# Token tiles kept apart at the stage borders, with four buffers for the split weights

## The chip, the cores and the metric

The kernel runs on one core of a Trainium2 chip. The metric is the device time of one execution in microseconds (us), the median of the runs shown. TensorE (PE) multiplies, VectorE (DVE), ScalarE (ACT) and GpSimd (POOL) do the element-wise work, and SyncE (SP) starts the loads of the weights.

## The reference, cut to what matters

Two networks run one behind the other on 256 tokens of width 1024, all in float32.

```python
h = x
h = h + mamba2_mixer(rms_norm(h, g_pre[0]), ...)            # 32 heads, state 128, then w_out 2048 x 1024
k_nope, k_rope, v = mla_shared_kv(h, ...)                   # ckv, then kv_up 256 x 2048
cq, gate = split(rms_norm(h, g_pre[1]) @ w_in, [384])
q = (rms_norm(cq, g_q) @ w_uq)                              # uq 384 x 1536, 16 heads of 64 + 32
h = h + (causal_attention(q, k, v) * silu(gate)) @ w_out    # mla_out 1024 x 1024
h = layer_norm(rms_norm(h, g_final), ln_in)
for l in range(2):
    q, k, v, u = h @ w_in[l]                                # qk 1024 x 1024, v and u 512 each
    a = softmax(q1 k1) - lam * softmax(q2 k2)               # 8 heads; a @ v, normed per head
    f = real(fft2(u)) per group of 128, @ w_f + b_f         # 4 groups
    h = layer_norm(ALPHA * h + concat(a, f) @ w_o[l], ln1)
    h = layer_norm(ALPHA * h + (silu(h @ w_g) * (h @ w_up)) @ w_down, ln2)   # width 2816
```

## The kernel before, in words

The tokens lie in two tiles of 128 (t = 0, 1; T is 2). The weights come as 134 units of 128 x 2048 numbers, in the fixed order of `unit_plan` (L66). SP loads a unit into one of RAW (4) slots of `raw` (L404). ACT copies it, rounded, to `whi` (L1097); DVE (L1485) and POOL (L2038) each subtract one half, which gives the remainder `wlo`. These three instructions are here called the split of a unit. `whi` and `wlo` have SPL (3) slots, so the split of unit u waits until PE has used unit u - 3 (`w_used`), and SP loads unit u once DVE and POOL have split unit u - 4. Each of the three engines calls `split.until(name)` at hand-placed points of its own program; that goes AHEAD (2) units past the name. A product is three matmuls: hi x hi, hi x lo, lo x hi. `streamed` (L447) runs a whole unit, 24 matmuls for a unit of full width: first 12 for tile 0, then 12 for tile 1. `turned` (L476) gives the transposed product of a unit, 48 matmuls of 256 columns.

The stages are: the projection and convolution of the Mamba block (12 units, L570), in which DVE works out dt (`dt_second`, L1576) for a small product at CUM_AT (L586); its scan over 16 pairs of heads (L699), in which z products (L606) fill in; its output units (`acc_units`, L716); the units ckv, cq, gate, kv_up and uq (L756 to L787); latent attention over 16 heads (L842); its four output units; then twice: the units vu and qk (L912), differential attention over 8 heads with the Fourier part behind it (L1017), the four w_o units, and 11 pairs of gu units with 11 down units (L1066).

Between two stages stands a border. The sum of the output units must be read from PSUM (`add_acc`, L1734), normed (for LayerNorm `moments` L1870 on DVE, `root_ln` on POOL, `affine` L1879), turned by PE (`turn_tile`, L873), split by ACT (L1150) and DVE (L1894), and only then can the next product of that tile start (`first_pair`, L882). Before, only the last output unit of a stage reports its tile 0 early (`acc_t0`); all others run both tiles. While it waits, PE runs `keep_busy(bank, n)` (L523), n products of ones whose results nobody reads; each shows as two records at L526. In differential attention PE has 48 pieces of real products, of three matmuls each, to fill in (`side_piece`, L921): 32 of qk and 16 of vu. ACT has for each head four exponentials (L1398), one copy of transposed probabilities (L1419), and the copies of the Fourier part (L1407 to L1411); DVE has the maxima (L1941) and the combination (L1954, L1957). The w_o products wait in `o_banks` (L1036) until DVE has read the attention result (L1988 to L1992). All transposes and Fourier products go in turn through two PSUM banks, TP, and each waits until the product before the last has been copied out (`fill`, L496).

## Time and profile before

| | us |
|---|---|
| median of 3 runs | 1064.04 (1064.04 to 1066.13) |
| the profiled execution | 1063.66 |
| its span | 1061.9 |
| PE busy in it | 989.2 |
| of that at L526 (products of ones) | 69.1 |
| ACT, DVE, POOL busy | 475.3, 526.9, 521.5 |
| chain that ended last: PE, DVE, ACT | 75%, 13%, 6% |

The profile gives each instruction's start and duration. Matmuls overlap, so the time from one start to the next says more of a matmul than its own duration. PEclk is the clock granted to TensorE as a share of 2.4 GHz.

### The profile page before, as it was taken

The numbers are of one execution on the slowest core, as the hardware profiler recorded it, in microseconds if no ns is written. First come the engines' busy times: TensorE is split into PE (matmuls) and PEld (weight loads), VectorE is DVE, ScalarE is ACT, GpSimd is POOL, SyncE is SP. The second block draws the span as 40 slices with busy tenths as digits, with TensorE's granted clock in tenths as the row PEclk, the third lists the DMA queues.
The fourth block names the chain that finished last, engine by engine and source line by source line (L and its number), as shares of the span: only waits on it lengthen the run. The fifth ranks groups of instructions, "written<-read, shape, count | busy, mean of one in ns | idle before, by whom it ended". The sixth has DMA issues, their size and how long they took to land.

```text
span 1061.9 us, 13606 instructions
## 1 busy us (share of the span) xinstructions
PE 989.2 (93%) x5100; PEld 802.0 (76%) x5100; DVE 526.9 (50%) x903; ACT 475.3 (45%) x747; POOL 521.5 (49%) x240
## 2 busy tenths in 40 slices
PE   8989899898988998998989999998998989999995
PEld 6979677686867975876767888886977757888884
DVE  4697765744346647375442232236275552222324
ACT  5655644544446732474324344333375323343440
POOL 5243752573633033652445665665552544656652
PEclk9999999999989999999999999999999999999998
DMA  9444221354443024422343555554422225545520
GB/s 371 183 159 159 106 94 41 119 195 153 168 138 140 2 99 156 181 81 80 119 142 136 198 189 198 173 194 158 165 108 85 83 92 182 189 168 198 191 87 40
DMA packets 21803, 151.77 MB, mean 143 GB/s; under 512 B 2544, under 2 KB 2928, under 8 KB 3824
## 3 DMA queue, kind: packets, MB, share of 16 engines
q1 hardware_dynamic: 19872, 142.62, 38.1%
q10 hardware_dynamic: 1872, 8.34, 2.1%
q8 instruction: 41, 0.67, 0.3%
q14 instruction: 18, 0.15, 0.0%
HBM read 149.90 MB, written 1.05 MB: 142 GB/s over the span
## 4 chain that ended last, share of the span: by engine, by line
PE 75%; DVE 13%; ACT 6%; issue 3%; POOL 2%; DMA 1%; SPq 0%; POOLq 0%; DVEq 0%; ACTq 0%
PE ps L464 16%; PE ps L470 15%; PE ps L466 15%; PE ps L946 3%; PE ps L488 2%; PE ps L492 2%; PE ps L490 2%; ACT whi L1097 2%; PE ps L508 2%; DVE wlo L1485 1%; PE ps L618 1%; PE ps L963 1%; DVE res L1885 1%; DVE small L1874 1%; DVE arena L1882 1%
## 5 line engine op out<-in xcount | busy, mean ns | idle before, releaser
L2038 POOL TENSOR_TENSOR wlo<-raw,whi 128x1024 fp32r<-128x1024 f32 x134 | 427.0, 3189 | 427.7 <-ACT whi L1097 427.7
L1097 ACT CAST whi<-raw 128x2048 fp32r<-128x2048 f32 x134 | 255.9, 1912 | 194.3 <-PE ps L470 169.7
L1485 DVE TENSOR_TENSOR wlo<-raw,whi 128x1024 fp32r<-128x1024 f32 x134 | 183.8, 1372 | 292.1 <-ACT whi L1097 291.7
L464 PE MATMUL ps<-whi,ahi 128*128 128x512 f32 (+1 forms) x432 | 168.6, 390 | 8.8 <-DVE arena L2014 7.8
L466 PE MATMUL ps<-wlo,ahi 128*128 128x512 f32 (+1 forms) x432 | 168.0, 389 | 0.0
L470 PE MATMUL ps<-whi,alo 128*128 128x512 f32 (+1 forms) x432 | 162.8, 389 | 0.0
L464 PE MATMUL ps<-whi,bhi 128*128 128x512 f32 (+1 forms) x322 | 128.7, 400 | 6.7 <-issue 3.6
L466 PE MATMUL ps<-wlo,bhi 128*128 128x512 f32 (+1 forms) x322 | 125.1, 388 | 0.0
L464 PEld LDWEIGHTS ps<-whi,ahi 128*128 128x128 f32 x432 | 81.5, 189 | 27.2 <-DVE arena L2014 9.1
L470 PE MATMUL ps<-whi,blo 128*128 128x512 f32 (+1 forms) x322 | 101.7, 389 | 0.0
L470 PEld LDWEIGHTS ps<-whi,alo 128*128 128x128 f32 x432 | 81.5, 189 | 16.5
L466 PEld LDWEIGHTS ps<-wlo,ahi 128*128 128x128 f32 x432 | 81.4, 188 | 16.1
L464 PEld LDWEIGHTS ps<-whi,bhi 128*128 128x128 f32 x322 | 61.4, 191 | 21.2 <-issue 5.2
L488 PE MATMUL ps<-ahi,whi 128*128 128x256 f32 x256 | 74.1, 290 | 0.4 <-POOL wlo L2038 0.4
L490 PE MATMUL ps<-alo,whi 128*128 128x256 f32 x256 | 73.1, 285 | 0.0
L492 PE MATMUL ps<-ahi,wlo 128*128 128x256 f32 x256 | 73.0, 285 | 0.0
L470 PEld LDWEIGHTS ps<-whi,blo 128*128 128x128 f32 x322 | 61.3, 190 | 12.7
L466 PEld LDWEIGHTS ps<-wlo,bhi 128*128 128x128 f32 x322 | 61.4, 191 | 11.9 <-issue 0.5
L526 PE MATMUL ps<-ones 128*128 128x512 f32 x146 | 69.1, 617 | 1.1 <-DVE neghalf L1514 1.1
L1136 ACT CAST bhi<-ps 128x512 fp32r<-128x512 f32 x26 | 15.0, 586 | 94.4 <-PE ps L508 94.4
L1496 DVE TENSOR_TENSOR blo<-ps,bhi 128x512 fp32r<-128x512 f32 x26 | 17.8, 690 | 75.4 <-ACT bhi L1136 75.4
L488 PEld LDWEIGHTS ps<-ahi,whi 128*128 128x128 f32 x256 | 49.8, 194 | 1.2 <-POOL wlo L2038 0.6
(261 smaller groups left out, 1586.4 us busy)
## 6 DMA issues: line engine op xcount, KB each, us to landing
raw<-in_wstream SPq DMA_DIRECT2D x134, 1024.0 KB, 4.8
par<-in_params ACTq DMA_DIRECT2D x5, 1024.0 KB, 5.1
tab<-in_tables ACTq DMA_DIRECT2D x1, 1352.0 KB, 8.6
res<-in_x SPq DMA_DIRECT2D x2, 512.0 KB, 4.4
out<-res SPq DMA_DIRECT2D x2, 512.0 KB, 2.6
wfs<-in_wf ACTq DMA_DIRECT2D x1, 512.0 KB, 11.3
par<-in_params ACTq DMA_DIRECT2D x1, 512.0 KB, 12.8
arena<-in_wsmall ACTq DMA_DIRECT2D x1, 256.0 KB, 8.6
```

The source lines that it names most:

```text
L464: pe.matmul(banks[t][b][:, 0:cw], h_, wh[:, i, c], start=st, stop=False, skip_group_check=True)
L466: pe.matmul(banks[t][b][:, 0:cw], h_, wl[:, i, c], start=False, stop=False, skip_group_check=True)
L470: mm = pe.matmul(banks[t][b][:, 0:cw], l_, wh[:, i, c], start=False, stop=last and i == nks - 1, skip_group_check=True)
L488: pe.matmul(o, wh[:, k, cc], ah[:, k, :], start=(k == 0), stop=False, skip_group_check=True)
L490: pe.matmul(o, wh[:, k, cc], al[:, k, :], start=False, stop=False, skip_group_check=True)
L492: mm = pe.matmul(o, wl[:, k, cc], ah[:, k, :], start=False, stop=(k == KT - 1), skip_group_check=True)
L508: tr = pe.transpose(bank[:, k * S + t * P:k * S + (t + 1) * P], src[:, t, c0 + k * P:c0 + (k + 1) * P], ident)
L526: pe.matmul(bank, ones[:, :], ones[:, :].unsqueeze(1).to_broadcast([P, 4, P]), start=True, stop=True)
L946: mm = pe.matmul(o, a, b, start=(first and j == 0), stop=(last and j == 2), skip_group_check=True)
L1097: act.copy(whi[:, u % SPL, :], raw[:, u % RAW, :]).then_inc(w_hi, 1)
L1485: dve.tensor_tensor(wlo[:, u % SPL, c], raw[:, u % RAW, c], whi[:, u % SPL, c].bitcast(F32), ALU.subtract).then_inc(w_lo_v, 1)
L2038: pool.tensor_tensor(wlo[:, u % SPL, c], raw[:, u % RAW, c], whi[:, u % SPL, c].bitcast(F32), ALU.subtract).then_inc(w_lo_p, 1)
```

## The change: what it does

Units: RAW goes from 4 to 3, SPL (two tiles a slot) from 3 to 4 and AHEAD from 2 to 3, which takes one slot more in all; `wfs`, the Fourier weights, moves into `arena` and is loaded once for each layer.

Borders: `streamed` is built on a new `tile_products(name, t, ...)` that runs one tile of a unit. The four mla_out units and the four w_o units run all of tile 0 first, then all of tile 1 (`skew` 4); so do the last three down units of each layer, with the last transposes of the hidden layer between them. Behind the border `lead_units` does the same with four units (vu 0 to 3; gu of j = 0 and 1), and the transposes of tile 1 stand ahead of its fourth unit. DVE and POOL norm tile 0 to its end before they take up tile 1, and make the splits that the next stage needs in between. The products of ones at the borders shrink.

Fill: all four vu units move ahead of differential attention, whose loop then has 32 side pieces, and the Fourier steps move from heads 6 to 9 to heads 3 to 8. In latent attention 36 pieces (uq 1, kv_up 1, uq 2, gate 2, gate 3) go before and into the loop of the heads, with copies by ACT, rotations by DVE and splits by all three in the same loop. In the scan each pair has two z pieces instead of three; the last 16 stand behind it, in the banks G[2] and G[3]. The work for dt is spread over more units, and CUM_AT goes from 6 to 7.

```diff
-RAW, SPL = 4, 3
-AHEAD = 2
-DT_AT, CUM_AT, CB_AT = 1, 6, 9
+RAW, SPL = 3, 4
+AHEAD = 3
+DT_AT, CUM_AT, CB_AT = 1, 7, 9
...
+A_PIECES = {-1: 6, 0: 10, 1: 14, 2: 17, 3: 20, 4: 25, 5: 30, 6: 36}
+
+A_SPLITS = {0: ("uq", 1), 2: ("kv_up", 1), 4: ("uq", 2), 6: ("gate", 2), 7: ("gate", 3)}
...
-    plan += [("ckv", 0), ("cq", 0), ("cq", 1)] + [("gate", i) for i in range(4)]
-    plan += [("kv_up", i) for i in range(2)] + [("uq", i) for i in range(3)]
+    plan += [("ckv", 0), ("cq", 0), ("cq", 1), ("gate", 0), ("gate", 1), ("kv_up", 0), ("uq", 0)]
+    plan += [("uq", 1), ("kv_up", 1), ("uq", 2), ("gate", 2), ("gate", 3)]
     plan += [("mla_out", i) for i in range(4)]
     for l in range(DEPTH):
-        plan += [("vu", l, 0), ("vu", l, 1)] + [("qk", l, i) for i in QK_ORDER]
-        plan += [("vu", l, 2), ("vu", l, 3)]
+        plan += [("vu", l, i) for i in range(4)] + [("qk", l, i) for i in QK_ORDER]
         plan += [("w_o", l, i) for i in (2, 3, 0, 1)]
...
-D_SPLITS = {1: ("qk", 3), 2: ("vu", 2), 4: ("vu", 3), 6: ("w_o", 2)}
+D_SPLITS = {1: ("qk", 1), 2: ("qk", 3), 3: ("w_o", 2)}
 
 
 def side_pieces(h):
 
 
-    return (0, 12, 22, 32, 36, 40, 44)[h + 2] if h < 5 else 48
+    return (0, 12, 22, 32)[h + 2] if h < 1 else 32
 
 
 def fourier_steps(h):
 
 
-    return {6: [("pq", 0), ("f", 0)], 7: [("pq", 1), ("fy", 0), ("f", 1)],
-            8: [("pq", 2), ("fy", 1), ("f", 2)],
-            9: [("pq", 3), ("fy", 2), ("f", 3), ("fy", 3)]}.get(h, [])
+    return {3: [("pq", 0)], 4: [("f", 0), ("pq", 1)], 5: [("fy", 0), ("f", 1), ("pq", 2)],
+            6: [("fy", 1), ("f", 2), ("pq", 3)], 7: [("fy", 2), ("f", 3)], 8: [("fy", 3)]}.get(h, [])
 
 
...
-                    if n > 3 * p:
-                        scan_head(2 * p + n - 3 * p - 1)
-                    z_piece(4 + n // 4, n % 4)
+                z_piece(4 + p // 2, 2 * (p % 2))
+                scan_head(2 * p)
+                scan_head(2 * p + 1)
+                z_piece(4 + p // 2, 2 * (p % 2) + 1)
+            for q in range(12, 16):
+                z_half(q)
             pe.wait_ge(e_done, SSM_HEADS)
             pe.wait_ge(int_read, SSM_GROUPS)
-            keep_busy(X[0], 5)
...
-            def acc_units(names, ah_of, first_wait):
+            def acc_units(names, ah_of, first_wait, skew=1):
 
                 first_wait()
-                for n, (name, kts, ready) in enumerate(names):
+                whole = len(names) - skew
+                banks = [[G[0], G[2]], [G[1], G[3]]]
+                for n, (name, kts, ready) in enumerate(names[:whole]):
                     ready()
                     ah, al = ah_of(n)
-                    streamed(name, ah, al, kts, 2, D, [[G[0], G[2]], [G[1], G[3]]], n == 0,
-                             n == len(names) - 1, acc_t0 if n == len(names) - 1 else None)
+                    streamed(name, ah, al, kts, 2, D, banks, n == 0, False)
+                for t in range(T):
+                    for n in range(whole, len(names)):
+                        name, kts, ready = names[n]
+                        if t == 0:
+                            ready()
+                        ah, al = ah_of(n)
+                        mm = tile_products(name, t, ah, al, kts, 2, D, banks[t], n == 0,
+                                           n == len(names) - 1)
+                        if t == T - 1:
+                            mm.then_inc(w_used, 1)
+                    if t == 0:
+                        mm.then_inc(acc_t0, 1)
 
 
             def y_ready(i):
                 if i == 0:
...
-            pe.wait_ge(ckv_read, 1)
-            for c in range(2):
-                for i in range(2):
-                    streamed(("gate", 2 * c + i), ahi, alo, range(4 * i, 4 * i + 4), 4, 512,
-                             [[(X, G)[c][0]], [(X, G)[c][1]]], i == 0, i == 1)
             pe.wait_ge(cn_done, T)
             turn_pair(("ckv", 0), cn, 0)
+            pe.wait_ge(ckv_read, 1)
+            for i in range(2):
+                streamed(("gate", i), ahi, alo, range(4 * i, 4 * i + 4), 4, 512, [[X[0]], [X[1]]],
+                         i == 0, i == 1)
             pe.wait_ge(qn_done, T)
             turn_pair(("cq", 0), qn, 0)
             turn_pair(("cq", 1), qn, 2 * P, 1)
             wait_emptied(pe, FILL["ckv", 0])
-            for u in range(2):
-
-                if u == 0:
-                    pe.wait_ge(gate_done, 2 * T)
-                    pe.wait_ge(qn_done, T)
+            streamed(("kv_up", 0), bhi, blo, (0, 1), 2, D, [[G[0], G[2]], [G[1], G[3]]], True, True)
+            wait_emptied(pe, FILL["cq", 1])
+            pe.wait_ge(gate_done, T)
+            streamed(("uq", 0), bhi, blo, (2, 3, 4), 3, 512, [[X[0]], [X[1]]], True, True)
+
...
-                if h == 0:
-                    pe.wait_ge(mc_read, 6)
-                    keep_busy(G[2], 4)
+                if h in A_PIECES:
+                    for n in range(A_PIECES[h - 1], A_PIECES[h]):
+                        part(n)
...
+            def lead_units(names, fills, banks, acc):
 
 
                 for t in range(T):
                     wait_emptied(pe, FILL[(*fills, t, 1)])
+                    pe.wait_ge(acc_read, T * acc + t + 1)
+                        if t == 0 and i == 3:
+                            turn_tile_when(fills, 1)
+                        mm = tile_products(name, t, ahi, alo, range(4 * (i % 2), 4 * (i % 2) + 4), 4, 512,
+                                           [banks[i // 2][t]], i % 2 == 0, i % 2 == 1)
...
-                keep_busy(X[0], (10, 4)[l])
+                keep_busy(X[0], 2)
                 turn_tile_when(("h", l), 0)
-                keep_busy(X[0], (2, 3)[l])
-                pe.wait_ge(acc_read, T * (2 + 2 * l))
-                first_pair([("vu", l, 0), ("vu", l, 1)], ("h", l), [G[2], G[3]])
+                keep_busy(X[0], 2)
+                lead_units([("vu", l, i) for i in range(4)], ("h", l), [[G[2], G[3]], [G[0], G[1]]],
+                           1 + 2 * l)
+                pe.wait_ge(u_done, T * l + 1)
                 turned(("qk", l, 0), ahi, alo, G[0])
+                pe.wait_ge(u_done, T * l + 2)
...
-                for kind, g in fourier_steps(NH + 1):
-                    fourier(kind, g)
 
                 def o_banks():
-                    pe.wait_ge(u_done, T * (l + 1))
+                    pe.wait_ge(qk_done, 4 * (l + 1))
...
-                          lambda n: (bhi, blo), o_banks)
+                          lambda n: (bhi, blo), o_banks, 4)
                 pe.wait_ge(ds_max, 2 * NH * (l + 1))
-                keep_busy(X[0], 4)
+                keep_busy(X[0], 2)
                 turn_tile_when(("hm", l), 0)
-                keep_busy(X[0], 3)
+                keep_busy(X[0], 2)
+                lead_units([("gu", l, j, i) for j in range(2) for i in range(2)], ("hm", l),
+                           [[X[0], X[1]], [G[0], G[1]]], 2 + 2 * l)
 
...
+                def last_ready(d):
+                    def ready():
+                        if d == FF_UNITS - 1:
+                            ff_turn(d)
                         wait_emptied(pe, FILL["ff", l, d])
-                        k0 = 2 * (d % 4)
-                        streamed(("down", l, d), bhi, blo, (k0, k0 + 1), 2, D,
-                                 [[G[0], G[2]], [G[1], G[3]]], d == 0, d == FF_UNITS - 1,
-                                 acc_t0 if d == FF_UNITS - 1 else None)
+                    return ready
+
+                for t in range(T):
+                    for d in range(FF_UNITS - 3, FF_UNITS):
+                        name, kts = down(d)
+                        if t == 0:
+                            last_ready(d)()
+                        mm = tile_products(name, t, bhi, blo, kts, 2, D, [G[t], G[2 + t]], False,
+                                           d == FF_UNITS - 1)
```

## Rows read from the trace of the kernel before

**Rows 1.** The page: engines, L526 and the splits (count, busy us, mean ns, idle before).
```profile
PE   989.2 (93%) x5100; PEld 802.0 (76%) x5100; DVE 526.9 (50%) x903; ACT 475.3 (45%) x747; POOL 521.5 (49%) x240
L526 PE MATMUL ps<-ones 128*128 128x512 f32 x146 | 69.1, 617 | 1.1 <-DVE neghalf L1514 1.1
L2038 POOL TENSOR_TENSOR wlo<-raw,whi 128x1024 fp32r<-128x1024 f32 x134 | 427.0, 3189 | 427.7 <-ACT whi L1097 427.7
L1097 ACT CAST whi<-raw 128x2048 fp32r<-128x2048 f32 x134 | 255.9, 1912 | 194.3 <-PE ps L470 169.7
```
**Rows 2.** Windows: length, PE, PEld, DVE, ACT, POOL busy, PEclk, DMA share, GB/s.
```profile
592.70:609.50 16.80, 16.80 (x78) 13.89 (x77) 5.02 (x6) 6.76 (x6) 10.28 (x4) 1.00 0.55 188
65.80:69.20 3.40, 3.37 (x17) 3.16 (x16) 3.30 (x14) 1.29 (x3) 0.00 (x0) 0.51 0.56 200
550.50:553.90 3.40, 3.40 (x10) 2.64 (x9) 1.23 (x1) 0.27 (x1) 3.05 (x1) 0.51 0.66 193
```
**Rows 3.** Timeline, dt: start, us, instruction, count, idle before it and its releaser.
```profile
64.93 0.41 PE L586 MATMUL ps<-small,tab 128*128 128x64 f32 x2 [3.53 <-DVE small L1592]
```
**Rows 4.** Windows of the scan and behind it, and two stretches of DVE's timeline.
```profile
116.00:182.90 66.90, 63.29 (x320) 48.20 (x320) 45.81 (x52) 32.34 (x74) 34.91 (x21) 1.00 0.27 95
184.00:197.80 13.80, 11.08 (x36) 5.10 (x35) 12.29 (x18) 9.78 (x23) 10.82 (x14) 0.92 0.21 76
115.20 7.48 DVE L1661 TENSOR_TENSOR arena<-arena 128x256 f32<-128x256 f32 x4
129.84 1.43 DVE L1661 TENSOR_TENSOR arena<-arena 128x256 f32<-128x256 f32 x4
```
**Rows 5.** PE's timeline before latent attention, and the window of its loop.
```profile
300.36 0.44 PE L508 MATMUL ps<-tab,arena 128*128 128x128 f32 x2 [1.94 <-DVE blo L1502]
310.30 0.50 PE L464 MATMUL ps<-whi,bhi 128*128 128x512 f32 x1 [2.40 <-ACT arena L1331]
320.12 0.47 PE L464 MATMUL ps<-whi,bhi 128*128 128x512 f32 x1 [2.44 <-issue]
336.14 3.60 PE L526 MATMUL ps<-ones 128*128 128x512 f32 x8
340.18:372.00 31.82, 31.11 (x252) 29.54 (x253) 19.58 (x78) 23.10 (x75) 0.05 (x1) 1.00 0.01 2
```
**Rows 6.** PE's timeline at the border behind mla_out.
```profile
400.38 8.75 PE L526 MATMUL ps<-ones 128*128 128x512 f32 x20
414.36 0.47 PE L894 MATMUL ps<-whi,ahi 128*128 128x512 f32 x1 [1.13 <-issue]
418.61 1.09 PE L879 MATMUL ps<-tab,res 128*128 128x128 f32 x8 [1.27 <-DVE res L1885]
```
**Rows 7.** Differential attention, layer 0: window from head 2, an ACT group, DVE.
```profile
456.67:501.90 45.23, 41.17 (x239) 32.13 (x238) 29.40 (x80) 29.05 (x71) 18.25 (x10) 1.00 0.27 94
L1398 ACT ACTIVATE arena<-arena,small 128x256 f32<-128x256 f32 x64 | 31.8, 498 | 28.9 <-DVE small L1941 28.8
496.51 0.69 DVE L1988 TENSOR_TENSOR arena<-ps,small 128x512 f32<-128x512 f32 x1 [2.61 <-PE ps L1007]
```
**Rows 8.** PE's timeline behind w_o, layer 0; the window there in layers 0 and 1.
```profile
524.68 3.60 PE L526 MATMUL ps<-ones 128*128 128x512 f32 x8
549.55 0.50 PE L464 MATMUL ps<-whi,ahi 128*128 128x512 f32 x1 [1.82 <-DVE arena L2014]
524.70:576.20 51.50, 44.11 (x183) 32.85 (x182) 22.14 (x26) 16.43 (x16) 23.41 (x11) 0.97 0.42 143
847.40:897.40 50.00, 42.63 (x183) 31.75 (x182) 22.20 (x26) 16.43 (x16) 23.51 (x11) 1.00 0.36 127
```
**Rows 9.** The end: window behind the last product, and DVE's tile 1 chain.
```profile
1048.90:1061.90 13.00, 0.02 (x1) 0.00 (x0) 8.05 (x11) 0.00 (x0) 3.77 (x4) 0.63 0.20 81
1052.53 1.28 DVE L1742 SCALAR_TENSOR_TENSOR arena<-res,ps 128x512 f32<-128x512 f32 x2
```
**Rows 10.** The tile `raw`: time from issue to landing of the 134 loads.
```profile
DMA to landing us min/median/max: 4.6/4.8/14.5
```

608 lines of the change are left out of this document (357 added, 251 removed).

## The prediction

> **What bounds the kernel now.** I read the page first: PE is busy 93% of the span, and no other engine more than half [rows 1]. So time goes only where PE waits, runs products of ones, or runs at the lower clock. The page gives the first two: 1061.9 - 989.2 = 73 us idle and 69 us at L526, 142 us in all. The reader should see that the second lies inside the 93%. Next I laid PE's timeline out with its idle times, and cut it at the borders [rows 3, 5, 6, 8, 9]. In the steady part of the hidden layer nothing is to be gained: 16.8 us, PE busy 16.8, clock 1.00 [rows 2]. This step also gives the price list. It has 72 matmuls and two pairs of transposes of some 0.35 us, so a matmul costs (16.8 - 0.35) / 72 = 0.228 us, a unit of 24 costs 5.5, one tile of it (12) 2.74, and a piece of three 0.69. Products of ones cost 8.75 / 20 = 0.44 us a record, 0.88 a call [rows 6]. Third, windows for the clock: it falls to half (1.2 GHz) in five stretches of 3.4 us inside the work, of which the first and the last are shown [rows 2]. PE is busy throughout, so one costs 1.7 us. Ahead of the five PE had idled 3.53 us [rows 3], 1.94 and 2.40 us [rows 5], 1.82 us [rows 8], and a part of the 13.8 - 11.08 = 2.7 us behind the scan [rows 4].
>
> **The change part by part.** All against the profiled execution. "E" is the end of the products of a stage.
>
> *Convolution and dt.* PE waits 3.53 us for dt [rows 3] and pays 1.7 us of clock behind it [rows 2]. The work for dt is now spread over three units of 5.9 us, and its result is due one unit later; what DVE does per unit then stays below the 5.9. Gain 5.2 us, at worst 3.
>
> *Scan.* The window has PE busy for 63.3 of 66.9 us and DVE for 45.8 [rows 4]. 16 z pieces go out of it, 16 x 0.69 = 11.0 us, which leaves PE 52.3 us. Now DVE is at 45.8 / 52.3 = 88%, and its sequence is in order: the reading of each group of heads waits for PE, and the masks behind it wait for that. So I add 7 us of stalls (the window had 3.6; bounds 3 and 12). Then come the 11.0 us of z pieces, in which all norms fit, and the way from the first turned block to the first output unit, 197.8 - 188.9 = 8.9 us, plus two products of ones and a wait, 10.2 us. Sum 52.3 + 7 + 11.0 + 10.2 = 80.5 against 81.8 us from 116.0 to 197.8. With the clock's fall to 0.92 in that stretch [rows 4] gone (0.9 us), gain 2.2 us; bounds -3 and +6.
> The masks (L1661) show what the feeding engines do to each other: four take 1.43 us when POOL rests, and 7.48 us beside POOL's products [rows 4]. The Trainium skill (GPSIMD Engine Reference, section 1, Specifications) says that GpSimd's way into SBUF is shared with VectorE, and that a VectorE instruction with two SBUF inputs contends with it. The trace agrees: 1.87 us each against 0.36. By that rule this change packs more such pairs into the scan and the borders; it is the second rival below.
>
> *Up-projections and latent attention.* Gone are waits of 1.94 + 2.40 + 2.44 us [rows 5] and some 1.2 us of smaller ones, 3.6 us of ones [rows 5], and two slow stretches of 1.7 us. That is 15.0 us. The loop of heads ran with PE busy 31.1 of 31.8 us and ACT 23.1 [rows 5], so 1.45 us of ACT and 2.0 of PE per head. ACT gets in: five splits of 1.9 us [rows 1] and some 4 us of copies. PE gets 30 pieces for heads 0 to 6, 2.8 to 4.2 us each, which cover them; the last split (head 7) has no piece over it, and ACT is held at head 6 by the last gate product. There PE waits 2.5 us; with the start of the loop 4 us of new waits (bounds 1 and 8). Gain 11.0 us. The border ahead of mla_out gains 0.9: its wait of 1.1 us goes, though ACT has a table load and the gate's silu more there.
>
> *Border behind mla_out.* From E to the first product 414.36 - 400.38 = 14.0 us. Now tile 0 is summed at E - 11.0 (four units of 2.74). Its chain is about 12 us (sum, square, root, scale, moments, two passes of 1.3 us, with one split between), so the transposes are ready at E + 1.8, behind two products of ones. ACT must take the square of tile 1 first, DVE its sum: first product at E + 6.1. The wait for tile 1's transposes, 1.27 us [rows 6], hides behind 11 us of tile 0. Gain 7.9 + 1.3 = 9.2 us.
>
> *Differential attention, each layer.* From head 2 on the window has 45.2 us, PE busy 41.2 [rows 7]. 48 matmuls (11 to 12 us) are moved ahead of the loop; they are work and stay in the sum. What is left to PE is 29.6 us. ACT has from there 12 groups of two exponentials, 2 x 0.498 us each [rows 7], 8 copies of 0.5, four Fourier steps of 1.35 and three splits of 1.9 [rows 1]: 11.9 + 4 + 5.4 + 5.7 = 27 us, all in order. So ACT is at 91%, and the two TP banks tie PE to it: I followed the heads one by one and found PE waiting 1.2 to 3 us in heads 4, 5 and 6, 6.8 us in all (bounds 3 and 12; before, the window had 4.1 us of idleness in all). At the end the Fourier steps no longer cover DVE's six passes of 0.69 (L1988 to L1992, the first in [rows 7]): `o_banks` holds PE for 4.3 us. 29.6 + 6.8 + 4.3 = 40.7 us against 45.2, of which 11.0 are moved work: a loss of 6.5. One wait of 1.0 at the loop's start goes, one of 0.6 comes for the turned attention blocks, and behind 4.3 us of idleness the clock falls, 1.7 us, as it did behind 3.53 us and less. Rounded over the pair of layers, loss 2 x 7.1 = 14.2 us (bounds 6 and 24).
>
> *Border behind w_o.* Before, the window of 51.5 us [rows 8] holds 9.5 us from E to the first product, three gu pairs (33 us), and waits of 1.3, 1.8 and 2.1 us. Now: first product at E + 4.8 (two calls of ones, transposes, two calls), 22 us of products and 1.1 of transposes, 0.6 + 11.0 + 0.6: 40.1 us. Gain 11.4 in layer 0, and 9.9 in layer 1, where no slow stretch stood.
>
> *End of the hidden layer.* The last down unit needs its input at once behind its transposes. ACT 0.59 and DVE 0.69 with their hand-overs are bare: 1.4 us each layer, loss 2.8.
>
> *Border to layer 1.* 9.5 us become 4.8, and a wait of 1.3 hides: gain 6.0.
>
> *The end.* 13.0 us follow the last product [rows 9]; DVE takes up tile 1 at 1052.53, 3.6 us after it, since tile 0 is still in work. Now tile 0 ended 8 us earlier. Gain 3.5.
>
> **The sum.** 5.2 + 2.2 + 11.0 + 0.9 + 9.2 - 14.2 + 11.4 + 9.9 - 2.8 + 6.0 + 3.5 = 42.3 us. Span 1061.9 - 42.3 = 1019.6; with the 1.8 us that lie around the span (1063.66 - 1061.9) it gives 1021.4. The median of the runs is 0.4 us above the profiled execution, within their spread, so I say 1021.5.
>
> **The rivals.**
> (1) *The loops are dense.* PE's queue of small products rides over ACT's order, and the clock holds. Then the scan has 3 us of stalls, attention 3 a layer and no fall: 4 + 7.6 + 3.4, and 2 us in latent attention, 17 us less: 1004 to 1012. For it: PE was busy 97% in the latent loop [rows 5]. Against it: ACT at 91% in order.
> (2) *The feeding engines become the bound.* DVE and POOL get in each other's way as in [rows 4] at each border and in both kinds of loops: the scan at its bound of 12 (+5), attention at 12 a layer (+10), latent attention +4: 1040. For it: the masks at 1.87 us. Against it: each border has several us of slack behind the transposes.
> (3) *The clock.* PE gets fewer products of ones. It fell behind a wait of 1.82 us in layer 0, and the same stretch of layer 1 kept 1.00 [rows 8]. Five more falls at the new waits of heads 4 to 6 and of the last down units would cost 5 x 1.7 = 8.5: 1030. The Trainium skill (TensorE: Matmul & The Clock Gate, "Why this matters for your kernels") warns against idle gaps between bursts of matmuls for this reason; by it the wait at `o_banks` is the one to fear, and it is in the sum.
> (4) *Slower than before: three raw slots.* A unit can be loaded only when the unit three before it is split. In the steady step three units take 16.8 us; ACT 1.9 + POOL 3.2 [rows 1] + start 0.4 + landing 4.8 [rows 10] are 10.3, so 6.5 us of slack. From a landing of 11.3 us on it binds, in some 18 steps; to eat 42 us it would have to reach 11.3 + 42 / 18 = 13.6 us in the middle, and any more makes the kernel slower, say 1070. The longest landing seen is 14.5, the median 4.8.
> (5) *It does not do what it says.* The chain of tile 0 takes as long as ever because in-order engines wait for tile 1 or a split first; the borders keep 9.5 to 14 us. Then 27 us of gain are gone: 1048.
>
> **How the numbers follow.** My forecast (1012 to 1033, the clock's case (3) within it) 0.68; dense 0.13; feeders 0.13; no early chain 0.04; three slots 0.02. The range takes in most of (1) and (2): 1007 to 1040, which leaves out some 15 in 100. A measurement of this kernel can tell about 0.2%, 2 us. Faster 0.97, same 0.01, slower 0.02.
>
> **What would show it.** Right: L526 falls from 146 to about 98 records; PE's first lead product comes 6 us behind mla_out and 5 behind w_o and the hidden layer; no wait at L586; a wait of 4 us ahead of the first w_o product with the clock at half behind it; waits of 1 to 3 us at the Fourier products; 9.5 us behind the last product. Wrong: a loop of attention at PE 97%, or of over 50 us; a scan window with more than 12 us idle; POOL's splits late at the lead units; idle of PE that ends with the loads of `raw`.

## The result: 0.6% slower, and where the 48 us went

Runs side by side on one chip gave 1069.97 us for the kernel after (median) and 1063.22 for the kernel before: ratio 1.0059, 95% interval 1.0046 to 1.0072. One of the 15 executions of the kernel after, at 1950.36 us, was a slow one and is not in the ratio. The forecast was 1021.5. The profiled execution of the kernel after has a span of 1068.2 us, against 1061.9 before, where I had worked out 1019.6. So 48.6 us are missing.

The page of the kernel after, and two groups of instructions by line:

```profile
span 1068.2 us, 13550 instructions
PE 988.7 (93%) x5052; PEld 813.8 (76%) x5052; DVE 558.1 (52%) x917; ACT 475.8 (45%) x748; POOL 522.7 (49%) x240
...
PEclk9999999999989999988999999999899898999998
...
L1595 DVE TENSOR_TENSOR wlo<-raw,whi 128x1024 fp32r<-128x1024 f32 x134 | 209.3, 1564 | 233.7 <-ACT whi L1166 233.2
...
L532 PE MATMUL ps<-ones 128*128 128x512 f32 x98 | 47.8, 623 | 1.1 <-DVE neghalf L1624 1.1
```

The products of ones went from 146 records to 98, as forecast, and from 69.1 to 47.8 us [rows 1]. Yet PE is as busy as before, 988.7 us. The 21 us that the ones gave back are in the other matmuls, which are the same ones: they ran slower. The mean granted clock is 0.960, and was 0.987.

I cut PE's timeline of both kernels at the same events (each stretch goes from the start of its first instruction to the start of the next stretch's). The 48 matmuls moved in each layer (48 x 0.228 = 10.9 us) are taken out of the stretch that got them, and stretches that changed by less than 0.2 us are left out:

| stretch, us | before | after | gain | forecast |
|---|---|---|---|---|
| start, convolution and dt (to the first z piece) | 103.78 | 101.91 | +1.9 | +5.2 |
| scan, y turns, mixer's first output units | 140.37 | 135.03 | +5.3 | +2.2 |
| up-projections and latent attention | 119.38 | 112.30 | +7.1 | +11.9 |
| mla_out: last product to first lead product | 13.98 | 8.08 | +5.9 | +7.9 |
| to the first scores, layer 0 / 1 (less 10.9) | 25.72 / 25.72 | 33.45 / 30.94 | -7.7 / -5.2 | +1.3 / +1.3 |
| attention and w_o, layer 0 (plus 10.9) | 84.60 | 94.35 | -9.8 | -7.1 |
| attention and w_o, layer 1 (plus 10.9) | 84.62 | 94.40 | -9.8 | -7.1 |
| behind w_o to the steady hidden layer, 0 / 1 | 51.54 / 49.97 | 48.91 / 48.92 | +2.6 / +1.1 | +11.4 / +9.9 |
| hidden layer, 0 / 1 | 151.36 / 151.51 | 153.08 / 153.24 | -1.7 / -1.7 | -1.4 / -1.4 |
| hidden layer's last product to the next layer's first | 9.51 | 7.18 | +2.3 | +4.7 |
| behind the last product | 13.0 | 9.4 | +3.6 | +3.5 |

The largest misses are in two kinds of stretch, each in both layers: from the lead units to the scores (9.0 and 6.5 us), and from w_o to the steady hidden layer (8.8 and 8.8 us). In each stands a wait that my sum has no line for. The first, on PE's timeline and then on ACT's (columns: start, duration, engine, line, operation, count, idle time before it and its releaser):

```profile
423.67 0.55 PE L494 MATMUL ps<-ahi,whi 128*128 128x256 f32 x1 [3.83 <-DVE wlo L1595]
```

```profile
409.00 0.59 ACT L1492 COPY arena<-ps 128x512 f32<-128x512 f32 x1 [2.46 <-PE ps L471]
419.88 0.58 ACT L1492 COPY arena<-ps 128x512 f32<-128x512 f32 x1 [10.29 <-PE ps L471]
420.36 5.50 ACT L1166 CAST whi<-raw 128x2048 fp32r<-128x2048 f32 x3
```

Four lead units hold all four split buffers, and `w_used` counts only in their pass of tile 1. The first buffer comes free at some 411 us (PE ends the first lead unit's tile 1 there). But ACT stands at its copy of tile 1 of u, which wants the last lead product, and waits 10.29 us. Three splits follow at once, and the turned unit behind them is 3.8 us late. The second wait, behind the first gate-and-up pairs:

```profile
556.95 0.79 PE L465 MATMUL ps<-whi,ahi 128*128 128x512 f32 x1 [3.06 <-DVE arena L2170]
557.54 0.63 PE L467 MATMUL ps<-wlo,ahi 128*128 128x512 f32 x1
```

The pair j=2 writes the banks of j=0, but waits for `gu_done` up to j=1, and the last product of j=1 has ended only 3 us before. The matmuls behind it take 0.63 us instead of 0.39. Windows of the kernel after, behind five waits (columns as in [rows 2]):

```profile
424.00:430.00 6.00, 6.00 (x31) 6.00 (x31) 5.91 (x2) 1.86 (x2) 6.00 (x3) 0.53 0.46 171
498.00:501.00 3.00, 3.00 (x8) 2.32 (x8) 1.43 (x3) 0.00 (x0) 2.37 (x2) 0.50 0.00 0
529.20:532.00 2.80, 2.80 (x7) 2.22 (x8) 2.73 (x5) 0.97 (x1) 1.33 (x2) 0.50 0.56 234
557.50:562.00 4.50, 4.50 (x12) 3.48 (x11) 1.29 (x1) 0.13 (x1) 3.67 (x2) 0.50 0.87 335
731.40:735.00 3.60, 3.60 (x16) 3.00 (x17) 3.53 (x5) 0.00 (x0) 2.13 (x2) 1.00 0.43 182
```

The clock (the column ahead of the last two) is at half (1.2 GHz) behind waits of 3.8, 4.3, 2.5 and 3.1 us, and full behind one of 2.7 us. Half clock makes the 96 turned matmuls 14.4 us long instead of 11.7 (in the kernel before), and the 48 of pair j=2 13.9 instead of 11.0.

### The profile page after: what moved, and what is told of

Read it like the earlier page. It is cut to its first block, busy times and chain, and to the rows that moved or that the text cites. A ratio compares the mean times of both kernels' runs of the same rounds, so it can differ in the third digit from the quotient of the medians.

```text
span 1068.2 us, 13550 instructions
## 1 busy us (share of the span) xinstructions
PE 988.7 (93%) x5052; PEld 813.8 (76%) x5052; DVE 558.1 (52%) x917; ACT 475.8 (45%) x748; POOL 522.7 (49%) x240
## 4 chain that ended last, share of the span: by engine, by line
PE 76%; DVE 11%; ACT 6%; issue 3%; POOL 2%; DMA 1%; SPq 0%; POOLq 0%; DVEq 0%; ACTq 0%
PE ps L465 16%; PE ps L467 15%; PE ps L471 15%; DVE wlo L1595 3%; PE ps L494 3%; ACT whi L1166 3%; PE ps L496 3%; PE ps L498 3%; PE ps L996 2%; PE ps L514 2%; DVE res L2018 2%; PE ps L532 2%; PE ps L1013 1%; PE ps L1026 1%; PE ps L628 1%
## 5 line engine op out<-in xcount | busy, mean ns | idle before, releaser
L2196 POOL TENSOR_TENSOR wlo<-raw,whi 128x1024 fp32r<-128x1024 f32 x134 | 417.6, 3121 | 351.8 <-ACT whi L1166 351.5
L1595 DVE TENSOR_TENSOR wlo<-raw,whi 128x1024 fp32r<-128x1024 f32 x134 | 209.3, 1564 | 233.7 <-ACT whi L1166 233.2
L465 PE MATMUL ps<-whi,ahi 128*128 128x512 f32 (+1 forms) x512 | 204.5, 399 | 16.4 <-DVE alo L2027 10.3
L467 PE MATMUL ps<-wlo,ahi 128*128 128x512 f32 (+1 forms) x512 | 202.0, 395 | 0.0
L471 PE MATMUL ps<-whi,alo 128*128 128x512 f32 (+1 forms) x512 | 196.9, 395 | 0.0
L465 PE MATMUL ps<-whi,bhi 128*128 128x512 f32 (+1 forms) x302 | 120.4, 399 | 13.9 <-issue 10.2
L465 PEld LDWEIGHTS ps<-whi,ahi 128*128 128x128 f32 x512 | 98.6, 193 | 40.6 <-DVE alo L2027 13.6
L467 PEld LDWEIGHTS ps<-wlo,ahi 128*128 128x128 f32 x512 | 98.8, 193 | 19.8
L471 PEld LDWEIGHTS ps<-whi,alo 128*128 128x128 f32 x512 | 98.2, 192 | 20.4
L496 PEld LDWEIGHTS ps<-alo,whi 128*128 128x128 f32 x256 | 52.5, 205 | 0.2 <-issue 0.2
```

What stands on the lines that cost most here:

```text
L465: pe.matmul(banks[b][:, 0:cw], h_, wh[:, i, c], start=st, stop=False, skip_group_check=True)
L467: pe.matmul(banks[b][:, 0:cw], h_, wl[:, i, c], start=False, stop=False, skip_group_check=True)
L471: mm = pe.matmul(banks[b][:, 0:cw], l_, wh[:, i, c], start=False, stop=last and i == nks - 1, skip_group_check=True)
L496: pe.matmul(o, wh[:, k, cc], al[:, k, :], start=False, stop=False, skip_group_check=True)
L1595: dve.tensor_tensor(wlo[:, u % SPL, c], raw[:, u % RAW, c], whi[:, u % SPL, c].bitcast(F32), ALU.subtract).then_inc(w_lo_v, 1)
L2196: pool.tensor_tensor(wlo[:, u % SPL, c], raw[:, u % RAW, c], whi[:, u % SPL, c].bitcast(F32), ALU.subtract).then_inc(w_lo_p, 1)
```

## The experiments

Theory: the waits come from an order that ACT and PE keep although buffers and banks are free, and each wait is paid a second time in clock. Rivals: three raw slots; the early tile is worth nothing; DVE and POOL hold each other up. Times are medians; stretches and waits are those of each run's profiled execution; the ratio is to the kernel before on the same chip.

### Fill the waits with ones

```diff
                 pe.wait_ge(u_done, T * l + 1)
+                keep_busy(X[0], 4)
                 turned(("qk", l, 0), ahi, alo, G[0])
...
+                            if j == 2:
+                                pe.wait_ge(gu_done, T * (FF_UNITS * l + 1))
+                                keep_busy(X[0], 3)
...
+                    pe.wait_ge(ds_max, 2 * NH * (l + 1))
+                    keep_busy(X[0], 4)
                     pe.wait_ge(do_ss, T * (l + 1))
```

The calls of ones behind the transposes of tile 0, in places left out here, go from 2 to 6, 5 and 4.

> The kernel after, with more products of ones in six places where PE waits without them: 4 calls ahead of the first turned qk unit of each layer, 3 ahead of the gate-and-up pair j=2, 4 ahead of the first w_o unit, and 6 instead of 2 (mixer), 5 instead of 2 (hidden layer) behind the transposes of tile 0. No wait gets shorter by it; only TensorE's clock can change. Theory 'clock': the falls to 0.5 at these places (394, 423, 497, 529, 557 us and the same of layer 1) go, which the profile of after prices at 1.7 to 1.8 us for a product stretch of the border, 14.4 - 12.0 = 2.4 for the turned units, 4.7 - 2.8 = 1.9 at w_o, 13.9 - 11.0 = 2.9 behind the pair: 1.8 + 2 x (2.4 + 1.9 + 1.6 + 2.9) = 19, so about 1051 us. Rival 'waits alone': the clock falls anyway, or what it gives back is waited for by the next unit: 1066 to 1070.

Measured 1058.27 us, 0.9954 (0.9933 to 0.9975): 11.7 us less than the kernel after, clock 0.987. No wait was taken away, so these 11.7 us are clock alone. By stretches: 2.2 and 1.8 us from the lead units to the scores, 4.1 in each layer from gu to the steady state (where the lead units and pair j=2 were both slow). At w_o the held clock brought nothing: 24.41 against 24.53 us, for a wait of 1.4 us for the turned attention blocks now stands inside w_o; and behind mla_out tile 1's transposes waited 1.4 us instead of 0.4. These are a part of what is missing from the 19 expected: a slow stretch ahead of another wait is free.

### Let pair j=2 wait for the banks it overwrites

```diff
-                            pe.wait_ge(gu_done, T * (FF_UNITS * l + j))
+                            pe.wait_ge(gu_done, T * (FF_UNITS * l + (1 if j == 2 else j)))
```

> The kernel after, with one count changed: the gate-and-up pair j=2 waits until the banks of pair j=0 have been read (these are the ones it overwrites), and no longer for those of j=1. Theory 'needless wait': the 3.06 us at 553.9 us and the 2.9 us of half clock behind it go in both layers: -12 us, about 1058 us. Rival 'split buffers': unit (2,0) or (2,1) or the turned blocks of the hidden layer are the next thing that is late, since four buffers were held until 545 to 553 us; then a wait on wlo or whi stands in the same place and the time is 1066 or more.

Measured 1058.58, 0.9937 (0.9914 to 0.9960). The stretch from gu to the steady state takes 36.1 and 35.9 us instead of 41.9. The wait was needless, and nothing else was late there.

### Put the two qk splits ahead of ACT's copy

```diff
                     else:
+                        split.until(("qk", l, 2), 0)
                         made(act, ("vu", l, 3))
```

> The kernel after, with ACT's splits of the first two qk units put ahead of its copy of tile 1 of u (the copy waits for the last product of the lead units; the splits wait only for the first and the second of them in tile 1). Theory 'order on ACT': the wait of 3.8 us ahead of the first turned unit and the 2.4 us of half clock behind it go, 2 x 6.2 = 12.4 us, about 1058 us. Rival 'three raw slots and four held buffers': the raw units or the buffers come too late in any order, the wait stays at 2 us or more and the clock falls all the same: 1065 to 1070.

Measured 1058.25, 0.9934 (0.9912 to 0.9957). ACT's timeline now:

```profile
415.26 1.91 ACT L1166 CAST whi<-raw 128x2048 fp32r<-128x2048 f32 x1 [2.19 <-PE ps L471]
417.98 1.92 ACT L1166 CAST whi<-raw 128x2048 fp32r<-128x2048 f32 x1 [0.81 <-PE ps L471]
423.37 0.59 ACT L1493 COPY arena<-ps 128x512 f32<-128x512 f32 x1 [3.47 <-PE ps L471]
```

The splits wait for PE's release of a buffer, 0.8 to 2.2 us, and not for data: three raw slots suffice at this place. PE's wait ahead of the turned unit is gone.

### Both, without ones, and with

> The kernel after with the two edits of gate_wait and qk_splits_first and no more ones. Theory 'independent, and the clock at w_o costs nothing': they add up to 11.4 + 11.7 = 23.1, 1047 us, since the half clock at w_o is taken back by a wait for the turned attention blocks behind it (w_o's 24.5 us at half clock against 24.4 at full). Rival 'every fall costs its 1.7 us': combined1 had 1045.5 with the clock held at w_o and at three borders, which is 8.8 us by the prices of each, so this one comes to 1054.

Measured 1046.66, 0.9856 (0.9824 to 0.9888): 23.3 us less than the kernel after, where the two alone gave 23.1. They are independent.

> The kernel after with three edits together: the gate-and-up pair j=2 waits for the banks of j=0 alone; the first two qk splits stand ahead of the copy of tile 1; and 5, 5, 4 and 5 calls of ones fill the waits ahead of w_o, and behind the transposes of tile 0 (mixer, w_o, hidden layer). The two first measured 11.4 and 11.7 us alone. Theory 'independent': they add up, and the ones give back the clock at w_o and at three borders, 1.8 + 2 x (1.9 + 1.6) = 8.8 us at most: 1070 - 23 - 8.8 = 1038 us (1036 to 1042). Rival 'one feeder behind all': both waits came from the same late splits, so what one edit takes away the other finds again further on: 1050 or more.

Measured 1045.53, 0.9824 (0.9792 to 0.9856). The ones at w_o and at the borders are worth 1.1 us beside the two edits, not 8.8, and the intervals cannot tell that from nothing.

### The early tile itself: undo it

```diff
-                      lambda n: (ahi, alo), lambda: pe.wait_ge(o_gated, 2 * T), 4)
+                      lambda n: (ahi, alo), lambda: pe.wait_ge(o_gated, 2 * T))
...
-                          lambda n: (bhi, blo), o_banks, 4)
+                          lambda n: (bhi, blo), o_banks)
```

> The kernel after, with the mixer's output units and w_o in the order of the kernel before: three units with both tiles, only the last one split into tile 0 and tile 1. This undoes one part of the change, at three of the four borders. Theory 'the early tile is worth what its chain gains': the first lead product comes about 14 us instead of 8.1 us behind the mixer's last product and 9.5 instead of 7.0 us behind w_o: 5.9 + 2 x 2.5 = 11 us slower than the kernel after, about 1081 us. Rival 'held split buffers eat it': with three of the four units released one after the other, the splits of the lead units come evenly, and the time is within 3 us of the kernel after, 1067 to 1073.

Measured 1098.16, 1.0338 (1.0298 to 1.0378): 28 us slower than the kernel after, much more than the 11 expected; either expectation missed. The first lead product now comes 16.2 us behind mla_out and 15.0 behind w_o, later than in the kernel before (14.0 and 9.5). PE at the first of them:

```profile
397.97 1.97 PE L946 MATMUL ps<-tab,res 128*128 128x128 f32 x8 [8.91 <-DVE res L2018]
```

So with the splits and fewer ones as they now stand, tile 0's head start carries all three borders: 8.1 + 8.0 + 8.0 = 24 us.

### The lead units in two pairs

```diff
-                for t in range(T):
...
+                for pair in range(2):
+                    for t in range(T):
...
+                            if pair == 0 and t == 0 and i == 1:
+                                turn_tile_when(fills, 1)
```

With it ACT's copy of tile 0 of u, like that of tile 1, waits for the last lead unit.

> The kernel after, with the four lead units done in two pairs (tile 0 and tile 1 of the first two, then of the last two) instead of all four through tile 0 first. Two split buffers come free 11 us after the first product instead of four between 13.7 and 22. Theory 'held buffers': the wait for wlo ahead of the turned units falls from 3.8 us to under 1, and its half clock with it, 2 x 6 us; but tile 1's transposes are wanted 2.7 us behind the first lead product instead of 8.2, and they come 10.4 us behind it now, so PE waits 5 to 8 us at each of four borders: 1075 to 1090 us. Rival 'pairs are enough': tile 1's chain is ready soon after, and the time falls to 1055 to 1062.

Measured 1095.32, 1.0311 (1.0284 to 1.0337). Slower than either expectation. PE waits 7.4 us for tile 1 at the mixer and 3.4 to 4.7 us at the other borders. The wait for wlo did not go as expected: it is 4.3 us, since both of ACT's copies still stand ahead of the splits. So the pairs pay at the transposes and get nothing for it, and this run cannot say what an earlier release is worth. That the four held buffers do not make the wait by themselves is shown by qk_splits_first, which holds them as long and has no such wait: what was at fault was the order on ACT.

### Three raw slots, in the kernel before

```diff
-RAW, SPL = 4, 3
+RAW, SPL = 3, 3
```

> The kernel before with three raw slots instead of four, and nothing else (three split buffers as before). Rival 'three raw slots' of the prediction: a unit can be loaded only when the third one ahead of it is split; if that is what costs the kernel after its gain, the kernel before loses tens of us by it, 1090 or more. Theory 'raw slots have slack': landing 4.8 us, splits 1.9 and 3.2 us and start 0.4 us against 16.8 us for three units, so 0 to 5 us slower: 1063 to 1068.

Measured 1062.55, 0.9994 (0.9975 to 1.0012). In the kernel before three slots cost nothing. The kernel after with four was not run. In its trace ACT waits for loads of `raw` 11 times, 26.7 us in all and 4.9 at most, against one wait of 2.0 us before, so the slots are tighter; but loads are 1% of the chain that ended last in both kernels. The rival is out as the main cause.

### Tile 0 first on ACT and DVE

```diff
-                    lambda: split.until(("vu", 0, 2), 0))
+                    lambda: (split.until(("vu", 0, 2), 0), tile_hi(("h", 0), 0)))
...
                 for t in range(T):
-                    tile_in(t)
                     if t == 1 and turned_as:
                         tile_lo(turned_as, 0)
+                        split.until(splits[2], 0)
+                    tile_in(t)
```

> The kernel after, with the split of tile 0 (ACT's and DVE's part of the turned blocks) ahead of the sum and square of tile 1 at all four borders, and one of the two DVE splits behind it. Theory 'in-order engines': the first lead product comes 2.9 us earlier behind the mixer (8.1 to about 5.2 us behind its last product) and 1.5 to 2 us earlier at the three other borders; the waits fall below 1.5 us there and the clock with its 1.7 us holds at 2 or 3 of the 3 borders where it fell: 8 us of waiting and 3 to 5 of clock, 1057 to 1061 us. Rival 'tile 1 pays': what tile 0 gains, the transposes of tile 1 wait for, or the gate-and-up wait behind it: 1066 to 1070.

Measured 1068.29, 1.0041 (1.0019 to 1.0063): no more than 2 us, as the rival had it. The first lead product did come 5.4 us behind mla_out (8.1) and 4.3 behind w_o and the hidden layer (7.0, 7.2), somewhat earlier than in my sum (6.1 and 4.8). At the mixer all of it was lost again: PE waited 5.0 us for wlo of the fourth lead unit, whose split stands behind DVE's chain of tile 1. At the other borders tile 1's transposes were 1.8 us late. Once tile 0 is early, tile 1's chain is the bound.

> Against combined1 (1045.5 us): at the borders behind w_o and the hidden layer DVE splits the turned blocks of tile 0 ahead of the sum of tile 1. Alone on the kernel after the first lead product came 2.7 us earlier by it, and tile 1's transposes then waited 1.8 us. Theory 'tile 1's chain is next': net 0.9 us a border, 3 borders, 1042 to 1044 us. Rival 'the first product counts': 2.7 us a border, 1037 to 1039.

Measured 1044.25, 0.9816 (0.9788 to 0.9845), only 1.3 us from combined1, less than the intervals can tell.

### DVE beside POOL

```diff
-                c = slice(0, UW // 2)
+                c = slice(0, 3 * UW // 4)
...
-                c = slice(UW // 2, UW)
+                c = slice(3 * UW // 4, UW)
```

> The kernel after, with one size changed: DVE makes three quarters of each unit's low part and POOL one quarter, instead of half and half. POOL's operation then takes about half of 3.1 us and DVE's own, alone, 1.22 x 1.5 = 1.8 us. Theory 'the two hold each other up': in the profile of after small DVE operations beside POOL's subtraction take 2 to 2.3 us instead of 0.2, and DVE's splits 3.4 instead of 1.2; with POOL's part halved these delays are halved, DVE's mean split stays near 1.9 to 2.2 us, and the chains of the borders end 1 to 2 us earlier each: 1062 to 1067 us. Rival 'DVE's own length counts': 134 x 0.6 = 80 us more on an in-order DVE, the borders and the scan get later, 1075 or more.

Measured 1060.63, 0.9966 (0.9945 to 0.9988): 9.3 us less, a little more than the 3 to 8 expected. In the profiled execution, at 1056.93 the second fastest of ten, the first product behind w_o comes 2.6 us earlier in each layer, and each stretch behind it is 2.7 us shorter. The second pass of the norm, in groups by line of the kernels before, after and pool_quarter:

```profile
L1885 DVE SCALAR_TENSOR_TENSOR res<-arena,small,par 128x1024 f32<-128x1024 f32 x10 | 12.8, 1285 | 5.3 <-POOL small L2058 5.1
```

```profile
L2018 DVE SCALAR_TENSOR_TENSOR res<-arena,small,par 128x1024 f32<-128x1024 f32 x10 | 29.2, 2923 | 6.7 <-POOL small L2216 6.7
```

```profile
L2018 DVE SCALAR_TENSOR_TENSOR res<-arena,small,par 128x1024 f32<-128x1024 f32 x10 | 20.4, 2041 | 6.7 <-POOL small L2216 6.7
```

My chain of 12 us had two passes of 1.3 us. In the kernel after the second takes 2.9 us in the mean, because it now runs while POOL subtracts. POOL and then DVE in the kernel after, behind mla_out:

```profile
384.05 1.45 POOL L2216 TENSOR_TENSOR small<-small,neghalf 128x1 f32<-128x1 f32 x1
385.47 2.36 POOL L2196 TENSOR_TENSOR wlo<-raw,whi 128x1024 fp32r<-128x1024 f32 x1
```

```profile
385.60 3.31 DVE L2018 SCALAR_TENSOR_TENSOR res<-arena,small,par 128x1024 f32<-128x1024 f32 x1 [0.54 <-POOL small L2216]
```

The pass waits for POOL's small result (L2216), and POOL goes straight on to a subtraction, 0.13 to 0.15 us ahead of DVE. That is so at the eight passes at the borders, 3.31 to 3.35 us each; the two at the end, where POOL has nothing left to split, take 1.28, and so do all ten in the kernel before, none of which meets a subtraction.

> The kernel before, with the low parts divided three quarters (DVE) to one quarter (POOL), as in pool_quarter. Theory 'the change packed DVE's chains beside POOL's splits': in the kernel before the second pass of the norm takes 1.28 us in the mean, in the kernel after 2.92; so the kernel before has little to gain from a shorter POOL operation, 0 to 3 us: 1061 to 1064. Rival 'the split ratio was bad in both': it gains 9 us as the kernel after did, 1055.

Measured 1062.22, 0.9985 (0.9964 to 1.0005). In the kernel before there is nothing to gain that the runs can tell: it is the change that brought DVE's chains beside POOL's splits.

> tile0_first_ln (1044.3 us) with POOL's quarter, POOL's bias ahead of the split, and one call of ones fewer behind the transposes at w_o and at the hidden layer. Theory 'feeders': POOL's quarter gives its 9 us here as well, for it shortens the chains of both tiles at all borders, and the order on POOL another 3 to 9: 1027 to 1033 us. Rival 'the same time twice': the chains it shortens are covered by then, 1036 to 1042.

Measured 1046.24, 0.9829 (0.9788 to 0.9871).

> combined_quarter with POOL's part an eighth and DVE's seven eighths. DVE's own operation grows by some 0.3 us (1.22 us for half a unit), 134 x 0.3 = 40 us on an engine that is busy half of the time; POOL's shrinks again. Theory 'feeders': what a POOL operation holds up goes down with its length, 1 to 4 us less than combined_quarter. Rival 'DVE's length': from here on each split on DVE is as long as what it avoids, 0 to 5 us more than combined_quarter.

Measured 1044.87, 0.9815 (0.9780 to 0.9850). For the quarter both expectations missed. The eighth is 1.4 us less, inside the range of 'feeders', but the intervals cannot tell it from nothing. At w_o's border combined2 (below), which has the halves and is else the same there, is as quick: 4.8 us to the first product and 36.4 behind it, against 4.8 and 36.9. There the shorter POOL operation shortens nothing that PE waits for. From the end of mla_out to the scores of layer 0 it does: 44.1 us in combined_quarter against 47.0 in combined2. But both lost time between the first z piece and the first output unit, 95.6 and 97.1 us against 89.5 in pool_quarter, though combined_quarter does the same work in the same order there. The same window of combined_quarter and of pool_quarter:

```profile
126.40:140.80 14.40, 13.68 (x39) 10.21 (x40) 6.00 (x17) 4.17 (x10) 2.97 (x3) 0.53 0.21 73
```

```profile
126.40:140.80 14.40, 14.40 (x77) 10.93 (x77) 11.07 (x22) 7.34 (x21) 8.00 (x6) 1.00 0.21 75
```

The clock was at half for most of 14 us in the one and full in the other. Up to there the two run alike, 1.7 us apart: PE waits for the same operation of DVE until 127.12 and 125.41 us. In pool_quarter a slow stretch came ahead of this wait (mean clock 0.80 from 118.0 to 126.4 us), and 0.8 us of wait were left; in combined_quarter the clock was full there, PE waited 2.4 us, and the slow stretch came behind. Why it came when it did stays open. So these two runs do not price the quarter in the combined kernel, and combined2 with it was not run.

### The attention

```diff
-    return {3: [("pq", 0)], 4: [("f", 0), ("pq", 1)], 5: [("fy", 0), ("f", 1), ("pq", 2)],
+    return {6: [("pq", 0), ("f", 0)], 7: [("pq", 1), ("fy", 0), ("f", 1)],
...
```

> The kernel after, with the Fourier steps in the heads where the kernel before has them (6 to 8, and the last group behind the last head), where they cover DVE's reading of the attention's output. Theory 'ACT and DVE in order are the bound of heads 3 to 6': the 4.3 us ahead of w_o and the 1.9 us of half clock go, 12 us in both layers, but heads 3 to 5 have nothing left for PE and wait as long as now or longer: 1058 at best, 1062 to 1068 likely. Rival 'the steps were only badly placed': the waits of 2.8 and 2 x 1.4 us at the Fourier products and the fall of the clock at 462 us go too, 1048 to 1054.

Measured 1069.70, 1.0065 (1.0041 to 1.0090). The wait ahead of w_o fell from 4.3 to 0.6 us and w_o to 23.4 us, but the loop grew from 58.9 to 61.3: PE waits 1.3 us for ACT's copy, 2.4 us for DVE's maxima and 0.8 us for DVE once more (layer 0), and the clock is at half from some 460 to 481 us. The sum is no smaller. That fits a loop as long as the in-order chain on ACT and DVE, as the prediction had it; it does not prove it.

```diff
-D_SPLITS = {1: ("qk", 1), 2: ("qk", 3), 3: ("w_o", 2)}
+D_SPLITS = {1: ("qk", 1), 4: ("qk", 3), 6: ("w_o", 2)}
```

> Against combined1 (1045.5 us): the three groups of splits inside the attention loop stand at heads 1, 4 and 6 instead of 1, 2 and 3. Theory 'splits crowd heads 3 and 4': the wait of 2.8 us ahead of head 4's scores, which ends with DVE's maxima after POOL's bias and two splits beside each other, goes with the clock's 1.7 us behind it: 1038 to 1042 us. Rival 'ACT's and DVE's order alone': the split only moves its 1.9 us to a later head, where it holds up the same chain: 1043 to 1048.

Measured 1053.30, 0.9907 (0.9881 to 0.9934), worse than either expectation. The 2.8 us ahead of head 4's scores stayed, and the splits in the late heads cost 1.9 us (layer 0) and 5.8 us (layer 1) of the loop.

```diff
-                    if h - 2 in D_SPLITS:
+                    if h - 3 in D_SPLITS:
```

> Against combined1 (1045.5 us): POOL does its subtractions for the w_o units one head later, so that the bias of head 4 stands ahead of them. Theory 'order on POOL': in the trace of after the scores of head 4 wait 2.8 us for DVE's maxima, these wait for POOL's bias, and it stands behind a split that itself waited 7.6 us for ACT; so the 2.8 us and the clock's 1.7 us behind go in each layer, 1037 to 1040 us. Rival 'ACT's order': ACT's own splits and exponentials set head 4 and the heads behind it, 1043 to 1047.

Measured 1042.78, 0.9805 (0.9768 to 0.9843). The wait went from 2.8 to 1.2 us, but one of 1.6 to 2.7 us at the next transposes (for ACT's copy) took its place: 58.0 and 57.7 us for the loop, against 58.7 and 60.4. Of the 60.4, 1.7 us are a fall of the clock behind a wait of 2.3 us, which layer 0 has too, without the fall. So the order on POOL is worth some 0.7 to 1 us a layer, and the 2.7 us between the medians lie within the intervals; ACT's order holds the rest.

### All that helped, in one kernel

```diff
+                    keep_busy(X[0], 3)
                     pe.wait_ge(dt_done, 1)
...
+            pe.wait_ge(uq_read, T)
+            keep_busy(X[0], 3)
             mla_turn(0)
```

> combined1 with POOL's bias first, DVE's split of tile 0 first at the borders behind w_o and the hidden layer (3 and 4 calls of ones there), and three calls of ones each ahead of the wait for dt and ahead of the first head of the latent attention, 3.0 us each. Theory 'small gains add up': 2.7 (POOL's order) + 1.3 (borders) + 3 (half clock behind dt and the first head), 1038 to 1040 us. Rival 'absorbed': the next wait takes them back, 1041 to 1044.

Measured 1038.40, 0.9771 (0.9752 to 0.9791): 2.3% faster than the kernel before, and 31.6 us faster than the kernel after, as expected. Its page:

```profile
span 1034.4 us, 13638 instructions
...
PE 985.2 (95%) x5098; PEld 802.6 (78%) x5098; DVE 557.0 (54%) x917; ACT 476.1 (46%) x748; POOL 520.0 (50%) x240
...
PEclk9999999999999999999999999999999999999999
```

## Why the prediction was wrong, step by step

*Convolution and dt: failed.* I wrote that what DVE does per unit stays below 5.9 us. DVE's timeline of the kernel after:

```profile
64.74 1.23 DVE L1595 TENSOR_TENSOR wlo<-raw,whi 128x1024 fp32r<-128x1024 f32 x1
65.88 2.43 DVE L1727 SCALAR_TENSOR_TENSOR arena<-ps,vec,arena 128x255 f32<-128x255 f32 x6
68.22 0.88 DVE L1707 SCALAR_TENSOR_TENSOR small<-small 128x64 f32<-128x64 f32 x3
```

The last steps of dt stand behind a split and six taps, and PE waits 3.05 us (3.53 before), one unit later. The 5.2 us were 1.9.

*Scan: better than forecast*, 5.3 against 2.2: the 7 us of stalls that I added for DVE at 88% did not come. Two waits of 0.4 and 1.8 us stand at its start, and one fall of the clock.

*Up-projections and latent attention: 7.1 of 11.9.* I gave the start of the loop 1.5 us, and it took 3.0, with half clock behind it; the heads behind the last piece wait 3.6 us in all, where I had 2.5.

*Border behind mla_out: right in kind, 8.1 against 6.1.* Tile 0's chain ended 2.7 us behind the last product instead of 1.8, for its second pass took 3.3 us instead of 1.3; and DVE split the turned blocks behind the sum of tile 1. Then the clock fell, 1.7 us, which the sum had not.

*The wait for tile 1's transposes "hides behind 11 us": wrong, but not decisive.* The transposes stand ahead of the fourth lead unit, 8.2 us behind the first product. At the mixer they hid, but for 0.4 us, because the first product was late and the clock at half; in tile0_first, with an earlier product, they came 1.8 us late at the other three borders.

*From the lead units to the scores, and behind w_o: this is the step that failed.* I costed the lead units by their matmuls and asked who waits for the tiles. I never asked what they hold: four buffers whose release ACT passes on in order, and banks that a count releases together. By the trace the waits of 3.8 and 3.1 us are worth 2 x (3.8 + 2.7) = 13.0 and 2 x (3.1 + 2.9) = 12.0 us with the clock behind them; the runs without them gave 11.7 and 11.4 us (1070 - 1058.3 and 1070 - 1058.6), and 23.3 together. That is half of the miss. The sum for the windows behind w_o ("0.6 + 11.0 + 0.6") contains no wait.

*Attention: the right mechanism, some 2.7 us a layer too small.* The forecast was a loss of 7.1, it was 9.8. My own terms do not add up to 7.1: 6.5 - 1.0 + 0.6 + 1.7 = 7.8, by which the sum would have been 1.4 us smaller. The 4.3 us at `o_banks` came as forecast, 4.32, and the half clock behind it. That half clock cost nothing by itself: without it (ones_in_waits) w_o takes 24.4 us instead of 24.5, because 1.4 us of waiting for the turned attention blocks take its place. The waits at the Fourier products were 1.43 us each, twice a layer, and 2.8 us at head 4's scores.

*Ends: right.* 1.7 a layer against 1.4; the tail 9.4 against 9.5.

Of the rivals, the clock's case had the right mechanism and a price of 8.5 us, but for other places (heads 4 to 6 and the last down units); measured by filling the waits it is 11.7, and it stands on top of the waits. The feeding engines' case (DVE beside POOL) is shown for the kernel after (9.3 us) and not for the kernel before. I had argued against it with slack behind the transposes; the chain ahead of them had none. These 9.3 us overlap with the rest: how much of them is left once the two waits are gone was not measured. I had listed "POOL's splits late at the lead units" as a sign of being wrong: the late split was the one to look for, but by ACT's order. The slower case by three raw slots is not borne out (before_raw3, and qk_splits_first without a wait for data); that its 1070 us is the measured time is an accident. What the chances missed is that several rivals can come true at once; I had treated them as exclusive.

Edits took 31.6 us out of the kernel after. What the profiled execution of combined2, its fastest, still lacks (span 1034.4 against the 1019.6 of the sum, 14.8 us) lies, by the same stretches, 9.3 us at the borders and in the units behind them, 3.3 in the attention, 2.9 in the up-projections, 1.6 at dt and 0.6 in the hidden layer, less 3.1 that the scan gained beyond the forecast. At the borders PE now waits 1.9 us (mixer), 1.0 (w_o) and 0.2 (hidden layer) for tile 1's transposes; that its chain could be shortened was not tried.

## What to carry to other kernels

When a pass over tiles is split so that one tile goes first, the buffers of every unit in it are held for the whole first pass: write down what each in-order engine has queued between the first release and the split that waits for it, and cost that line like any other. Check what each count in a wait really protects. Look at what POOL starts in the moment in which it hands DVE a result. And price a new wait of PE twice, by its length and by the half clock that can follow, unless another wait behind it takes that back.

## What the runs showed of the hardware

A small operation of DVE with two inputs in SBUF, started beside POOL's subtraction, ends when POOL's ends. DVE and then POOL in the kernel after:

```profile
469.29 1.99 DVE L2106 SCALAR_TENSOR_TENSOR small<-small 128x2 f32<-128x2 f32 x1
```

```profile
468.92 2.35 POOL L2196 TENSOR_TENSOR wlo<-raw,whi 128x1024 fp32r<-128x1024 f32 x1 [2.06 <-ACT whi L1166]
```

Two columns of work take 1.99 us instead of 0.22, and end at 471.28, POOL's at 471.27. The rotation of q shows the same: 2.29 us instead of 0.24, from 293.30 to 295.59, beside a POOL operation that ends at 295.49. The second pass of the norm ends 1.08 us behind POOL's, most of the 1.28 us that it takes alone. It is a block, not a slowdown. And it does not hold for an operation with an input in PSUM: of the maxima (L2093), 14 of 64 start inside a subtraction of POOL, and all take 0.41 to 0.43 us. The Trainium skill (SBUF — State Buffer, "SBUF: two separate sides") says that the pair of ports which the two engines share is locked for a whole instruction, and that a VectorE instruction with two SBUF inputs is among those that need it; these rows agree. By that rule, and with the 2.4 us of POOL's subtraction from these rows, the price of such a DVE operation is up to 2.4 us more (an estimate) wherever the two meet, whatever its own length: I had used the rule for the masks and not for the second pass of the norm.

The length of a wait does not say whether the clock falls behind it. In the kernel after it fell behind waits of 1.8 to 4.3 us, and the border of layer 1 kept it at 1.00 behind 2.7 us; in the kernel before it fell behind 1.82 us at 549.55 us ([rows 8], [rows 2]) and was 1.00 from 320.2 to 323.6 us, behind a wait of 2.44 us ([rows 5]). And two kernels with the same work and order up to there differed by 6 us in the scan through the clock alone.
